# The context's sum of squares moved from the second MLP into the first MLP and the second layer norm, and two double chunks of modulation weights moved into the recurrent layer

## The reference, cut to what matters

```python
def rmsnorm(x, g):
    y = xf * lax.rsqrt(jnp.mean(xf * xf, axis=-1, keepdims=True) + RMS_EPS)
    return y * g
def modulate(h, shift, scale):
    return h * (1 + scale) + shift
# first block, layers i = 0 (attention) and 1 (recurrent), D = 1024, 256 tokens
shift, scale, gate = split(silu(c) @ ada_w[i, 0] + ada_b[i, 0], 3)
y = mixer(x * (1 + scale) + shift)
x = layer_norm(DN_ALPHA * x + (1 + gate) * y)
shift, scale, gate = split(silu(c) @ ada_w[i, 1] + ada_b[i, 1], 3)
y = square(relu((x * (1 + scale) + shift) @ w1)) @ w2
x = layer_norm(DN_ALPHA * x + (1 + gate) * y)
# second block
mod_x = split(silu(c_2) @ ada_w_2 + ada_b_2, 6)
mod_c = split(silu(c_ctx_2) @ ada_w_2 + ada_b_2, 6)
hx = modulate(rmsnorm(x), mod_x[0], mod_x[1])
hc = modulate(rmsnorm(ctx), mod_c[0], mod_c[1])
```

## Time and profile before

| | us |
|---|---|
| median of 3 runs | 1496.63 |
| lowest and highest of them | 1496.12, 1498.65 |
| profiled execution | 1495.06 |
| its span in the trace | 1493.7 |
| TensorE matmuls busy in it | 1357.3 (91%) |
| VectorE busy | 1096.1 (73%) |
| ScalarE busy | 751.1 (50%) |
| TensorE's share of the chain of work that ended last | 66% |
| VectorE's and ScalarE's share of it | 22%, 7% |

### The profile page before, as it was taken

The page is one execution under the profiler, slowest core; times in us unless marked ns, Lnnn a source line. Parts: engine busy times, 40 slices in busy tenths (PEclk is TensorE's granted clock), DMA queues, the critical chain, the costliest instruction groups (busy, mean ns, idle before and its releaser), DMA issues.

```text
span 1493.7 us, 20983 instructions
## 1 busy us (share of the span) xinstructions
PE 1357.3 (91%) x7872; PEld 1186.4 (79%) x7872; DVE 1096.1 (73%) x1502; ACT 751.1 (50%) x956; POOL 0.4 (0%) x5
## 2 busy tenths in 40 slices
PE   6879799998999977999987899898699999999996
PEld 6778699997777766998986678898687787777884
DVE  5767678777697867686786757876566868788686
ACT  3432444453666674454433543443146757566563
POOL 0000000000000000000000000000000000000000
PEclk9969999999999988999999899999799999999999
DMA  8628686773677754756573252321075977878772
GB/s 332 231 104 312 196 309 247 279 277 144 214 277 268 262 190 155 289 208 215 184 252 115 92 183 71 100 71 40 1 239 174 349 250 274 279 240 325 240 258 104
DMA packets 84212, 311.90 MB, mean 209 GB/s; under 512 B 9488, under 2 KB 9712, under 8 KB 83504
## 3 DMA queue, kind: packets, MB, share of 16 engines
q1 hardware_dynamic: 82080, 298.88, 57.0%
q10 hardware_dynamic: 2032, 11.69, 2.4%
HBM read 309.49 MB, written 1.05 MB: 208 GB/s over the span
## 4 chain that ended last, share of the span: by engine, by line
PE 66%; DVE 22%; ACT 7%; DMA 3%; issue 2%; DVEq 0%; ACTq 0%; SPq 0%
PE ps L433 65%; DVE w_low L392 8%; DVE junk L392 4%; ACT w_high L392 3%; DMA ring<-stream 1%; DMA ring<-moe 1%; DVE t_one L392 1%; DVE r_two L392 1%; DVE rs L392 1%; DVE x L392 1%; ACT h_high L392 1%; DVE t_two L392 1%; PE ps L1032 1%; DVE y_experts L392 1%; DVE all L392 0%
## 5 line engine op out<-in xcount | busy, mean ns | idle before, releaser
L392 DVE TENSOR_TENSOR w_low<-ring,w_high 128x1024 fp32r<-128x1024 f32 x368 | 451.0, 1225 | 149.9 <-ACT w_high L392 120.0
L392 ACT ACTIVATE w_high<-ring 128x1024 fp32r<-128x1024 f32 x368 | 390.3, 1061 | 294.2 <-PE ps L433 173.6
L433 PE MATMUL ps<-x_high,w_high 128*128 128x256 f32 (+1 forms) x784 | 237.1, 302 | 34.4 <-DVE x_low L392 22.6
L433 PE MATMUL ps<-x_low,w_high 128*128 128x256 f32 (+1 forms) x784 | 233.9, 298 | 0.0
L433 PE MATMUL ps<-x_high,w_low 128*128 128x256 f32 (+1 forms) x784 | 233.7, 298 | 0.0
L433 PEld LDWEIGHTS ps<-x_high,w_high 128*128 128x128 f32 x784 | 155.5, 198 | 44.3 <-issue 16.1
L433 PEld LDWEIGHTS ps<-x_low,w_high 128*128 128x128 f32 x784 | 155.7, 199 | 2.5
L433 PEld LDWEIGHTS ps<-x_high,w_low 128*128 128x128 f32 x784 | 155.4, 198 | 2.8
L392 DVE CUSTOM_DVE_ANT_0 junk<-ring,cond 128x1024 f32<-128x1024 f32 x109 | 133.6, 1226 | 29.9 <-DMA ring<-stream 16.8
L433 PE MATMUL ps<-h_high,w_high 128*128 128x256 f32 x512 | 146.7, 287 | 6.6 <-DVE h_low L392 4.2
L433 PE MATMUL ps<-h_low,w_high 128*128 128x256 f32 x512 | 145.6, 284 | 0.0
(11 more groups left out here) (299 smaller groups left out, 2066.7 us busy)
## 6 DMA issues: line engine op xcount, KB each, us to landing
ring<-stream SPq DMA_DIRECT2D x376, 512.0 KB, 4.8
ring<-moe SPq DMA_DIRECT2D x192, 512.0 KB, 4.7
tab_two<-tab ACTq DMA_DIRECT2D x1, 2824.0 KB, 15.0
gw<-gw ACTq DMA_DIRECT2D x1, 2304.0 KB, 13.2
cond<-cvec ACTq DMA_DIRECT2D x3, 512.0 KB, 5.5
x<-xT ACTq DMA_DIRECT2D x1, 1024.0 KB, 11.7
ctx<-ctxT ACTq DMA_DIRECT2D x1, 1024.0 KB, 4.8
pos<-posT ACTq DMA_DIRECT2D x1, 1024.0 KB, 8.3
```

What stands on the lines that cost most here:

```text
L392: return op(*a, **k).then_inc(self.sem, 1)
L433: return pe.matmul(out, stationary, moving, start=start, stop=stop, skip_group_check=True)
```

## The change

- The squares of ctx are made in the first MLP. ctx is loaded a second time, early, into a place that is free then (`CTX0`); ScalarE makes one quarter of the squares after each of the turns 2 to 5, into `CTX_SQ`. TensorE sums them directly behind the sums of the second layer norm, into bank 7, and ScalarE takes the root (now the third of all roots) behind the eight copies of `x_whole`; VectorE's reciprocal goes to `RSTD_CTX`, ahead of the first `xcv`.
- In the second MLP the squares, the sums, TensorE's wait, the root and the reciprocal are gone. ctx * rstd and the eight modulating instructions stand together between t = 13 and t = 14; `lows` between t = 14 and t = 15.
- The double chunks 6 and 7 move from turn 14 into the recurrent layer, as the second chunks of blocks 13 and 15; `TWO_CHUNKS` gets 1 and 15. The stream's order follows: two pieces more in block 1's place and two more in block 15's.
- silu(c_ctx_2) gets a place of its own (`COND[2]`) and is loaded and computed together with silu(c_2) in the attention layer; before, it was loaded and computed at the recurrent layer's end.

```diff
-A2_TURNS = ((0,), (1,), (2,), (3,), (4,), (5,), (6, 7), ())
-A2_ORDER = [8, 9, 10, 11] + list(range(12, 18)) + list(range(8)) + list(range(18, 24))
-TWO_CHUNKS = (3, 5, 7, 9, 11, 13)
+A2_TURNS = ((0,), (1,), (2,), (3,), (4,), (5,), (), ())
+A2_ORDER = [8, 9, 10, 11, 12, 13, 14, 6, 15, 16, 7, 17] + list(range(6)) + list(range(18, 24))
+TWO_CHUNKS = (1, 3, 5, 7, 9, 11, 13, 15)
...
+        self.CTX0, self.CTX_SQ = kt(view("ctx_first", aB + 5120, 2048)), kt(view("ctx_sq", aB + 7168, 2048))
+        self.RSTD_CTX = self.RS[:, 256:512]
...
     layer_norm(1)
+    square_sums(SQ_CTX, PS[:, 7, 0:256], m.CTX_SQ, KT)
...
-    mlp(W_MLP1, 8, 4, x_splits(MOD_LN2) + 1)
-    square_sums(SQ_CTX, m.VAR, m.T2, KT)
-    pe.wait_ge(s.root, 4)
-    mlp(W_MLP1 + 32, 12, 4, None)
+    mlp(W_MLP1, 8, 8, x_splits(MOD_LN2) + 1)
...
     act.dma_start(m.CB[:, 1, :], cvec[1:2, :].broadcast_to([P, D])).then_inc(s.in_c2, 16)
+    act.dma_start(m.COND[2], cvec[2:3, :].broadcast_to([P, D])).then_inc(s.in_c2, 16)
...
     A(m.CB[:, 1, :], m.CB[:, 1, :], ACT.Silu, s.silu_c2)
+    A(m.COND[2], m.COND[2], ACT.Silu, s.silu_c2)
...
+    act.dma_start(m.CTX0, ctxT).then_inc(s.in_c2, 16)
     act.dma_start(m.GW, gw).then_inc(s.in_gw, 16)
-    mlp(W_MLP0, 0, 8)
+    mlp(W_MLP0, 0, 3)
+    act.wait_ge(s.in_c2, 48)
+    for i in range(4):
+        A(m.CTX_SQ[:, 2 * i:2 * i + 2, :], m.CTX0[:, 2 * i:2 * i + 2, :], ACT.Square, s.sq)
+        mlp(W_MLP0 + 8 * (3 + i), 3 + i, 1)
+    mlp(W_MLP0 + 56, 7, 1)
...
     shifted(MOD_LN1, m.combo[:, 32:40])
+    root(3, m.RSTD_CTX, PS[:, 7, 0:256], 1.0 / D, "eps6")
     next_x(1, range(8))
...
-    act.dma_start(m.CB[:, 0, :], cvec[2:3, :].broadcast_to([P, D])).then_inc(s.in_cc, 16)
     high_upto(W_MLP1 + 4)
-    act.wait_ge(s.in_cc, 16)
-    A(m.CB[:, 0, :], m.CB[:, 0, :], ACT.Silu, s.silu_cc)
...
-    rms_rows(m.CTX, KT, m.T2, D, 4, None)
...
+    vv.wait_ge(s.root, 3)
+    op(vv.reciprocal, m.RSTD_CTX, m.RSTD_CTX)
...
-    mlp(W_MLP1, 8, 4)
+    mlp(W_MLP1, 8, 6)
+    bias(144, 16, "ada_b2", 0)
     vv.wait_ge(s.in_late, 48)
-    rms_rows(4, m.CTX, m.CTX)
-    mlp(W_MLP1 + 32, 12, 3)
-    bias(144, 16, "ada_b2", 0)
+    op(vv.tensor_tensor, m.CTX[:, :, :], m.CTX[:, :, :], m.RSTD_CTX.unsqueeze(1).broadcast_to([P, KT, S]), ALU.mult)
     lows = modulate_norm(MOD_CTX, m.CTX, "n1g", 144, 152, 1)
+    mlp(W_MLP1 + 48, 14, 1)
     lows()
     mlp(W_MLP1 + 56, 15, 1)
```

More of the change, by code:

```diff
@@ L104 @@
 MCOL, MN = _cols([("tri", 128), ("slot", CAP), ("mine", 5)])
-SQ_LN, SQ_CTX, SQ_POS, SQ_FN, SQ_HY, SQ_MOE, SQ_END = (0, 4, 8, 16), 12, 20, 24, 25, 26, 30
+SQ_LN, SQ_CTX, SQ_POS, SQ_FN, SQ_HY, SQ_MOE, SQ_END = (0, 8, 12, 16), 4, 20, 24, 25, 26, 30
 def stream_order():
@@ L168 @@
 Sems = collections.namedtuple("Sems", """
-    x_pos in_rnn in_c in_c8 in_par in_x in_att in_c2 in_cc in_gw in_late in_filt in_sel out
+    x_pos in_rnn in_c in_c8 in_par in_x in_att in_c2 in_gw in_late in_filt in_sel out
     w_high w_low used ada ada_pe mod_set x_alpha
     act dve
-    lam_abs lam_exp silu_c8 silu_c silu_c2 silu_cc ones
+    lam_abs lam_exp silu_c8 silu_c silu_c2 ones
     t2 x_high x_low x_whole x_add x_scaled x_next sums
@@ L215, in __init__ @@
         self.KF = view("kf", aKF, 2048)
+        self.COND = (self.CB[:, 0, :], self.CB[:, 1, :], view("cond_ctx", aKF, 1024))
         place(P)
@@ L1214, in scalar_program @@
         A(m.X[:, 4 * h:4 * h + 4, :], m.X[:, 4 * h:4 * h + 4, :], ACT.Copy, s.x_alpha, scale=ALPHA)
-    act.wait_ge(s.in_c2, 16)
+    act.wait_ge(s.in_c2, 32)
     A(m.CB[:, 1, :], m.CB[:, 1, :], ACT.Silu, s.silu_c2)
+    A(m.COND[2], m.COND[2], ACT.Silu, s.silu_c2)
     high_upto(W_MLP0 + 4)
@@ L1283, in scalar_program @@
     scan_pair(NB // 2 - 1)
-    act.wait_ge(s.ada, 96 - len(E_PIECES))
-    act.dma_start(m.CB[:, 0, :], cvec[2:3, :].broadcast_to([P, D])).then_inc(s.in_cc, 16)
     high_upto(W_MLP1 + 4)
-    act.wait_ge(s.in_cc, 16)
-    A(m.CB[:, 0, :], m.CB[:, 0, :], ACT.Silu, s.silu_cc)
     layer_norm(2)
-    root(3, m.RSTD, m.VAR, 1.0 / D, "eps5")
+    root(4, m.RSTD, m.VAR, 1.0 / D, "eps5")
     shifted(MOD_LN2, m.combo[:, 32:40])
@@ L1303, in rms_rows @@
         root(eps_count, m.RSTD, m.VAR if sums is None else sums, 1.0 / norm, "eps6")
-    mlp(W_MLP1, 8, 4)
-    act.wait_ge(s.in_late, 48)
-    rms_rows(m.CTX, KT, m.T2, D, 4, None)
-    mlp(W_MLP1 + 32, 12, 3)
+    mlp(W_MLP1, 8, 7)
     modulated(MOD_CTX, 1)
@@ L1528, in modulation @@
                 col = ADA_COL[ada[0]] + off + j
-                op(vv.tensor_tensor_reduce, junk, m.piece(c), m.CB[:, v, :], 1.0, 0.0, ALU.mult, ALU.add, m.MOD[:, col:col + 1],
+                op(vv.tensor_tensor_reduce, junk, m.piece(c), m.COND[v], 1.0, 0.0, ALU.mult, ALU.add, m.MOD[:, col:col + 1],
                    inc=s.ada if n == len(conds) - 1 else None)
@@ L1758, in conditions @@
             return ((0, 0),)
-        return ((1, 0), (0, 48)) if col < 112 else ((1, 0),)
+        return ((1, 0), (2, 48)) if col < 112 else ((1, 0),)
     def mlp(w0, t0, turns):
@@ L1793, in vector_program @@
     next_x(range(8))
-    vv.wait_ge(s.silu_c2, 1)
+    vv.wait_ge(s.silu_c2, 2)
     op(vv.memset, m.XP[:, :, 0:2], 0.0)
     op(vv.memset, m.XP[:, :, 258:260], 0.0, inc=s.xp)
+    vv.wait_ge(s.root, 3)
+    op(vv.reciprocal, m.RSTD_CTX, m.RSTD_CTX)
     def z_of(b):
@@ L1847, in vector_program @@
     evacuate(1, W_MLP1, m.gate1)
-    layer_norm(2, 3, 80, 72, ALPHA)
-    vv.wait_ge(s.silu_cc, 1)
-    mlp(W_MLP1, 8, 4)
+    layer_norm(2, 4, 80, 72, ALPHA)
+    mlp(W_MLP1, 8, 6)
+    bias(144, 16, "ada_b2", 0)
     vv.wait_ge(s.in_late, 48)
-    rms_rows(4, m.CTX, m.CTX)
-    mlp(W_MLP1 + 32, 12, 3)
-    bias(144, 16, "ada_b2", 0)
+    op(vv.tensor_tensor, m.CTX[:, :, :], m.CTX[:, :, :], m.RSTD_CTX.unsqueeze(1).broadcast_to([P, KT, S]), ALU.mult)
     lows = modulate_norm(MOD_CTX, m.CTX, "n1g", 144, 152, 1)
+    mlp(W_MLP1 + 48, 14, 1)
     lows()
```

## The result

| | before | after |
|---|---|---|
| median, us | 1496.72 (1496.12 to 1501.33, 6 runs) | 1479.48 (1476.64 to 1481.06, 6 runs) |
| profiled execution, its span | 1495.06, 1493.7 | 1476.64, 1475.3 |
| mean granted clock | 0.954 | 0.960 |

The changed kernel takes 0.9876 of the time before, 95% interval 0.9860 to 0.9892. Two later medians of the same kernel are 1480.40 and 1480.05, which lie inside the range by 0.6 and 0.3 us. So which side of the range's end a median falls on is chance here.

The account below looks back on a forecast made before the run. TensorE, busy 91% of the span, was taken as the bound. 6.45 + 6.3 + 1.3 = 14.05 us off 1493.7 gives 1479.6, 1481.0 for the whole profiled execution, 1482.5 with 1.57 to the median; range 1479.8 to 1487.3.

Parts of the forecast that it names:

- Place 1: Second MLP, between turns 11 and 12: without the context's squares, sums, wait and root, 6.45 us gained; bounds 6.2 to 6.5.
- Place 2: Second MLP, turns 14 and 15: 7.0 us lost there, less 0.7 of stall, 6.3 gained; bounds 3.5 to 7.0.
- The stall ahead of turn 14: Second MLP: the context's work makes VectorE late, so TensorE waits 0.7 us; 0 to 3.5 possible.
- The recurrent layer: VectorE's eight added reduces, about 10.4 us, stay hidden: 0 us taken, bounds 0 to 4.8.
- The cover at block 15: Recurrent layer: VectorE's idle 4.58 us and a further 0.96 wait hide four reduces of 5.2 us, by 0.3 us.
- the sign that the prediction named: Recurrent layer: TensorE waiting for `ring` in blocks 1 to 3 or 14 would show the prediction wrong.
- The first MLP and ctx's early load: First MLP: ScalarE's four squares cost nothing; the 1 MB load taken as 0, with 2.5 us kept for the range.
- Place 3: Second norm: the new sums fill TensorE's 4.57 us gap, so z runs at full clock, 1.3 us gained; bounds 0 to 1.5.
- Behind the second MLP: From the second MLP's end to the span's end: the prediction's sum has no term here.
- The rival on the clock: Clock falls elsewhere: up to one more with the second norm's gain gone, 1485.5, or one fewer, 1480.8; chance 0.11.
- From span to median: Whole kernel: profiled execution of 1481.0 plus the 1.57 us by which the median of three runs lay above it, 1482.5.
- one fewer: Whole kernel: one fall of the clock less than forecast, giving 1480.8 us.

Follow-up runs that it names:

- the kernel with the chunks alone: Changed kernel with the context's squares, sums, root, reciprocal and ctx * rstd back between turns 11 and 12 of the second MLP: 1488.66 us, ratio 0.9935.
- the late double chunk: Changed kernel with double chunk 7 and single chunk 17 exchanged, putting four reduces at the recurrent layer's very end: 1480.15 us, ratio 0.9888.
- the kernel with the fill around the fourth norm: Changed kernel plus idle matmuls behind the second MLP only (6 ahead of the fourth norm, 9 between its sums, 10 behind): 1476.67 us, ratio 0.9865.
- the kernel with the gap filled: Kernel before plus eight idle matmuls behind the second norm's sums: 1494.55 us, ratio 0.9982.
- the fastest one: Changed kernel, recurrent layer's last modulation ahead of block 15's gates, idle matmuls in seven gaps and seven more ahead of block 14's products: 1469.61 us, ratio 0.9824.

## Why the prediction was right in its places and wrong in its size

- **Place 1, 6.45: right.** 668.12 to 721.73 took 53.61 us before; the same two turns take 47.16 after (663.91 to 711.07). Nothing new was late there.
- **Place 2, 6.3: right.** From the chain's entry for turn 14 to the end of the MLP (745.67 to 805.47 before, 734.64 to 788.11 after) 59.80 and 53.47 us, so 6.33. The stall ahead of turn 14 was 0.52 for 0.7, there is none at turn 15, and no fall of the clock. That the stall is the price of ctx * rstd is shown by the kernel with the chunks alone.
- **The recurrent layer, 0: right in the changed kernel's three executions, but the stream is thin.** The cover at block 15 held: the wait for `y` is 7.41 in both kernels. How thin the place is was shown by the late double chunk, which paid its 2.5 us in full. At blocks 3 and 4, behind the pieces that the change adds in block 1's place, the added weights are thin too. The stretch from z to the products of block 12 takes 187.61 us where nothing disturbs it. In five of the eleven executions of kernels with the moved chunks it is longer at a clock of 1.00, by 0.05, 0.1, 0.3, 0.35 and 0.75 us, each time in these blocks. The profile names the cause in the largest, the kernel with the fill around the fourth norm:

```profile
412.83 3.69 PE L438 MATMUL ps<-x_whole,ring 128*96 128x256 f32 x16 [0.52 <-DMA ring<-stream]
```

  That is the sign that the prediction named (TensorE waiting for `ring` in blocks 1 to 3), at a small price. None of the four executions without the moved chunks has it.
- **The first MLP and ctx's early load, 0: right** within what can be told: 203.97 before, 203.71 after, in the mean.
- **Place 3, 1.3 with bounds of 0 to 1.5: the step that failed.** The mechanism held (gap filled, z at full clock, 14.03 us for 14.1), but the price was read from a single execution, and its upper bound too. That execution was the cheapest of three with this gap: the fall cost 1.4, 1.5 and 2.6 us (64 matmuls in 15.47, 15.55 and 16.66 against 14.03), and in the medians of the kernel with the gap filled, 2.7 (0.9 to 4.3). The term was about 2.0, the mean of the kernel before's two executions, its bounds 1.4 to 2.6 at least. The rival on the clock named the draw, but priced it only as a loss of this gain (1.3) or as "one fewer" at 1.7; that a larger fall may already sit in the median before was left out.
- **Behind the second MLP, 0: missing from the sum.** Up to the fourth norm's second sums (VectorE adds the MLP's result to x, TensorE sums) the time is 0.5 us shorter in the mean, and this goes with the clock: the work lost to the low clock there (how it is counted stands at the document's end) is 2.7 and 2.7 us before, 1.7, 1.7 and 2.6 after, for 7.85 and 7.79, 7.18, 7.19 and 7.72 us. With two and three executions it may be chance. The rest of the span is 0.8 shorter, and this isn't the clock: all of it lies behind the router, 265 us later, where the change has no edit. There the kernel before takes 415.15 and 415.41 us, the changed one 414.62, 414.48 and 414.00, and all five lose 2.0 to 2.1 us to the low clock. The cause stays open.
- **From span to median.** The prediction set its sum on one profiled execution and added the 1.57 us to the median. The mean spans give 16.0 where the sum gave 14.05; the medians (1496.72 and 1479.48) give 17.2, since that of before lies 2.8 us above its mean span and that of after 1.6. With the later medians of the changed kernel it is 2.1 to 2.5. So a us or so is the draw of the runs that make a median.

So of the 3 us missed, 2.0 stand in the spans (0.7 place 3's price, 1.3 behind the second MLP, 0.4 in the second MLP's other turns, less 0.4 in the stretches that the change leaves alone), and about 1 is the draw. The prediction doesn't work out its low end; one fewer fall (1480.8) less what the upper bounds of the three places add (0.05 + 0.7 + 0.2) gives the 1479.8. With an upper bound of 2.6 at place 3 it would have been 1478.7 and held the time. What is shown of this is place 3's price, and that the 0.5 ahead of the fourth norm's second sums goes with the clock; the 0.8 behind the router is not explained.

## What to carry to other kernels

Work that TensorE waits for on its own path (sums of an input known from the start) is worth the whole wait when it moves into a gap that TensorE has anyway, and more if the gap was long enough to bring its clock down. Price such a gap from several executions, since a fall behind the same gap costs 1.4 us in one and 2.6 in the next. After each gain look at the next `y`: where another engine sets it, speeding TensorE up only makes a longer wait, and that wait may bring the clock down again, until it is filled too.

## What the runs showed of the hardware

- A wait of one length may or may not bring the clock down. TensorE in the second MLP's first turn, changed kernel, first and second execution:

```profile
612.32 0.39 PE L438 MATMUL ps<-h_high,w_high 128*128 128x256 f32 x1 [1.88 <-DVE h_low L397]
```

```profile
615.83 0.39 PE L438 MATMUL ps<-h_high,w_high 128*128 128x256 f32 x1 [1.89 <-DVE h_low L397]
```

  and the two stretches behind them, in the same order (columns as above; the first with all engines, PEclk is the third number from the end). In the first execution every stretch from 606 to 622 us has a clock of 1.00:

```profile
616.00:618.00 2.00, 1.70 (x14) 1.70 (x15) 1.79 (x5) 0.60 (x1) 0.00 (x0) 1.00 0.80 244
```

```profile
616.00:618.00 2.00, 2.00 (x11) 0.54 0.04 12
```

  The same kernel, the same wait, and the clock stayed at 1.00 in the one and was 0.54 in the other. The Trainium skill, page "TensorE: Matmul & The Clock Gate", Part 1 (the HAM clock gate), says that the gate's window runs freely of the program; the trace agrees.
- Idle matmuls of constants keep the clock up as well as real ones: behind either, z's 64 matmuls took 14.03 us and the stretch to the products of block 12 187.61.
- A stretch in which nothing comes late and the clock falls only behind its last wait repeats to the hundredth: 187.61 in eight executions of six kernels. What is longer has a fall at its start (1.4 to 2.6 us) or comes late at blocks 3 and 4 (0.05 to 0.75 us, a wait for the stream where the profile names one).
- The time lost to the low clock (TensorE's busy time in stretches below full clock, times one less the clock) is 50.2 us over the span of before, 44.1 to 48.0 in the changed kernel and 31.5 in the fastest one. Of the 12.6 to 16.5 us less, only 10.4 came out in the median (1480.05 to 1469.61), and 1.9 of these are the earlier `y`, which isn't the clock's. Where another engine sets the pace, the low clock cost nothing: the last `y` comes 10.43 us behind the one before whether the 32 matmuls between them take 9.69 us or 7.14.
